# Delta heads: ten products ahead of the first head, queries' bank emptied in hop 3, gate product and second half of the system matrix later

## What is computed

```python
def gated_deltanet(h, w_in, conv_w, a_log, dt_bias, o_norm_g, w_out):
    proj = h @ w_in                                  # queries, keys, values, gate per head
    qkv = silu(causal_dwconv(qkv, conv_w))           # four taps
    q = l2norm(q) * (GDN_DK ** -0.5);  k = l2norm(k)
    kk = einsum('bhcid,bhcjd->bhcij', kc, kc)
    tri = where(strict, b * kk * decay, 0) + eye     # the system matrix
    sol = triangular_solve(tri, rhs)                 # the kernel inverts tri
    def step(S, inp):                                # over the chunks, in order
        v_new = u_c - w_c @ S
        o = qd_c @ S + qk_c @ v_new
        S = cd_c * S + kd_c.T @ v_new
    o = rmsnorm(o, o_norm_g) * silu(gate)            # the gate product
    return o @ w_out
```

## Time and profile before

| what | value |
|---|---|
| median of three runs | 2954.01 us (2953.73 to 2957.56) |
| profiled execution, time | 2953.93 us |
| profiled execution, span | 2952.2 us |
| granted TensorE clock, mean | 0.996 |
| busy: PE, DVE, ACT, POOL | 98%, 72%, 43%, 24% |
| delta heads in the span | from 1660.84 us (first P4) on; 454.56 us from the P4 of head 1 to the P4 of head 7 |

### The profile page before, as it was taken

How to read it: one execution, slowest core, us unless ns; L and a number is a source line. 1 busy time by engine, 2 the same in 40 slices (tenths; PEclk the granted TensorE clock), 3 DMA queues, 4 the chain that set the end, 5 groups by cost and what they waited for, 6 DMA issues and landing times.

```text
span 2952.2 us, 41363 instructions
## 1 busy us (share of the span) xinstructions
PE 2902.3 (98%) x14190; PEld 2409.8 (82%) x14190; DVE 2131.2 (72%) x2591; ACT 1257.9 (43%) x1857; POOL 720.9 (24%) x1126
## 2 busy tenths in 40 slices
PE   8999999999999999999899999999999999999998
PEld 7888887878888888887787788888887888878887
DVE  6665669858686868687886666666665667788887
ACT  4121124345454545455445454455453433344444
POOL 1000000014444444445001322222221356630000
PEclk9999999999999999999999999999999999999999
DMA  4213236332111211122532211111112344465542
GB/s 108 93 58 99 85 80 217 117 100 58 46 50 43 64 46 50 44 63 89 200 129 52 90 40 40 39 39 39 39 53 75 117 159 153 151 230 164 157 157 86
DMA packets 346911, 274.34 MB, mean 93 GB/s; under 512 B 82232, under 2 KB 297272, under 8 KB 342976
## 3 DMA queue, kind: packets, MB, share of 16 engines
q1 hardware_dynamic: 345664, 273.05, 30.1%
q10 hardware_dynamic: 1152, 0.07, 0.0%
HBM read 197.80 MB, written 75.27 MB: 92 GB/s over the span
## 4 chain that ended last, share of the span: by engine, by line
PE 89%; DVE 5%; issue 2%; DMA 1%; POOL 1%; ACT 1%; SPq 0%; DVEq 0%; POOLq 0%; ACTq 0%
PE banks L1105 9%; PE banks L1107 9%; PE banks L1106 9%; PE banks L1003 5%; PE banks L1005 5%; PE banks L1004 5%; PE banks L1087 3%; PE banks L1088 3%; PE banks L1089 3%; PE banks L1499 3%; PE banks L1500 3%; PE banks L1498 3%; PE banks L1590 3%; PE banks L1592 3%; PE banks L1591 3%; PE banks L1132 2%
## 5 line engine op out<-in xcount | busy, mean ns | idle before, releaser
L1105 PE MATMUL banks<-state_a_hi,weights_hi 128*128 128x512 f32 x1280 | 539.7, 422 | 0.9 <-DVE weights_lo L2221 0.8
L1107 PE MATMUL banks<-state_a_hi,weights_lo 128*128 128x512 f32 x1280 | 504.0, 394 | 0.0
L1106 PE MATMUL banks<-state_a_lo,weights_hi 128*128 128x512 f32 x1280 | 501.0, 391 | 0.0
L1107 PEld LDWEIGHTS banks<-state_a_hi,weights_lo 128*128 128x128 f32 x1280 | 240.3, 188 | 54.4
L1105 PEld LDWEIGHTS banks<-state_a_hi,weights_hi 128*128 128x128 f32 x1280 | 241.6, 189 | 39.5 <-issue 2.0
L1106 PEld LDWEIGHTS banks<-state_a_lo,weights_hi 128*128 128x128 f32 x1280 | 242.3, 189 | 34.0 <-issue 0.5
L831 POOL TENSOR_TENSOR beta<-beta,stick_left 128x128 f32<-128x128 f32 (+1 forms) x192 | 169.5, 883 | 393.0 <-DVE stick_left L2458 391.0
L2458 DVE TENSOR_TENSOR_SCAN stick_left<-stick_left,eps_column 128x128 f32<-128x128 f32 (+1 forms) x192 | 237.1, 1235 | 29.5 <-POOL beta L826 23.1
L2221 DVE TENSOR_TENSOR weights_lo<-weights_raw,weights_hi 128x1024 fp32r<-128x1024 f32 x133 | 180.6, 1358 | 80.6 <-ACT weights_hi L1618 68.2
L1618 ACT ACTIVATE weights_hi<-weights_raw 128x1024 fp32r<-128x1024 f32 x133 | 140.1, 1053 | 194.2 <-PE banks L1005 155.7
L1003 PE MATMUL banks<-state_a_hi,weights_hi 128*128 128x512 f32 x536 | 208.8, 389 | 1.5 <-DVE stream_again L2756 1.5
(11 more groups left out here) (532 smaller groups left out, 7327.8 us busy)
## 6 DMA issues: line engine op xcount, KB each, us to landing
weights_raw<-in_mlp_w_dram SPq DMA_DIRECT2D x34, 512.0 KB, 5.6
weights_raw<-in_gdn_w_in_dram SPq DMA_DIRECT2D x33, 512.0 KB, 4.1
weights_raw<-in_pool_w_in_dram SPq DMA_DIRECT2D x32, 512.0 KB, 4.1
state_a_lo<-relu_blocks_dram SPq DMA_DIRECT2D x16, 1024.0 KB, 7.1
weights_raw<-in_sb_w_in_dram SPq DMA_DIRECT2D x32, 512.0 KB, 4.1
relu_blocks_dram<-relu_sums SPq DMA_DIRECT2D x16, 1024.0 KB, 4.3
state_b_lo<-relu_blocks_dram SPq DMA_DIRECT2D x16, 1024.0 KB, 8.8
down_weights_raw<-in_mlp_w_dram SPq DMA_DIRECT2D x30, 512.0 KB, 5.3
```

Of the source, the lines that this page charges most:

```text
L1105: pe.matmul(psum[:, bank, :], whi, hi, start=(k == 0), stop=False)
L1106: pe.matmul(psum[:, bank, :], whi, lo, start=False, stop=False)
L1107: last = pe.matmul(psum[:, bank, :], wlo, hi, start=False, stop=(k == end - 1))
```

## The change

1. PE, way in: the last two products of T2 come after the keys' sums of squares; T3's products around `scores_k` are cut 4 and 4 (6 and 2 before); T4's first four products come ahead of the queries' sums of squares, its other twelve behind; the transposed keys and the scores come after all of T4. `AHEAD` is 10: eight products of T5's first half and two of its second before P4. `IN_INVERSE` stays, so T6 (the gate) begins in hop 4 and hops 7 and 8 hold no product.
2. DVE and ACT, way in: order of evacuations, taps and rescalings changed to fit; ACT makes three small exponentials after the keys' norm instead of before.
3. DVE, every head: queries' first bank is emptied at n = 3 (5 before), with the wait for the keys' taps; the keys' second bank before the wait for the root of the output (n = 0 of the next head before).
4. DVE, every head: P1_4 of the next head stands between y1 and y2, and y2 has a semaphore of its own.
5. DVE, every head: NT1 is at n = 17 (15 before), behind St3.

```diff
-        AHEAD, IN_INVERSE = KC - 2, (2, 1, 2, 1, 2, 1, 1)
+        AHEAD, IN_INVERSE = KC + 2, (2, 1, 2, 1, 2, 1, 1)
...
-            return [(x // KC, x % KC) for x in range(2 * KC, 8 * KC)
+            return [(x // KC, x % KC) for x in range(AHEAD + sum(IN_INVERSE), 8 * KC)
...
-            gemm_part(base[0], 1, 0, KC, A)
+            gemm_part(base[0], 1, 0, 6, A)
...
-                    for k in range(AHEAD):
-                        gemm_part(tile_at[0], 0, k, k + 1, A)
+                    for x in range(AHEAD):
+                        gemm_part(tile_at[0], x // KC, x % KC, x % KC + 1, A)
...
             for h in range(2):
                 norm_sum("k", h, 7 - h)
+            gemm_part(base[0], 1, 6, KC, A)
             base[0] = tile.fixed
-            gemm_part(base[0], 0, 0, 6, A)
+            gemm_part(base[0], 0, 0, 4, A)
             for h in range(2):
                 scores_k(h, 7 - h)
-            gemm_part(base[0], 0, 6, KC, A)
+            gemm_part(base[0], 0, 4, KC, A)
             gemm_part(base[0], 1, 0, KC, A)
+            base[0] = tile.fixed
+            gemm_part(base[0], 0, 0, 4, A)
             for h in range(2):
                 norm_sum("q", h, 7 - h)
-            base[0] = tile.fixed
-            gemm_part(base[0], 0, 0, KC, A)
+            gemm_part(base[0], 0, 4, KC, A)
+            gemm_part(base[0], 1, 0, KC, A)
             turn_k()
             scores()
-            gemm_part(base[0], 1, 0, KC, A)
             head("first")
...
             act.preload_act_table_set(LN_EXP)
+            decays()
+            norm_roots("k", (7, 6))
+            decay_rows()
             act.wait_ge(pre_dve, PRE["dl"])
...
-            decays()
-            norm_roots("k", (7, 6))
-            decay_rows()
             split_weights(halves.value())
...
             square_rest("k")
-            dve.wait_ge(pre_act, PRA["eg"])
-            did("neg", dve.tensor_scalar(eg_s[:, :, :], eg_s[:, :, :], -1.0, None, ALU.mult))
-            after("neg")
-            evac(1)
-            tap(qT, 0, slice(0, 1))
+            rescale(2, 3)
...
+            def level_step(l):
+                ev.wait("pe", f"P{l}")
+                ev.did(f"P1_{l}", dve.tensor_tensor(P1[:, :, :], psum[:, 4, :].rearrange("p (c n) -> p c n", n=64),
+                                                   lmask[:, l - LEVEL0:l - LEVEL0 + 1, :].to_broadcast([P, TT, 64]), ALU.mult))
             def head(kind, e):
-                ev.next[0] = 0
+                ev.next[0] = 1
...
-                    if n == 0:
+                    if n == 9:
                         evac(1)
-                    if n in (5, 9):
-                        evac((n - 5) // 4)
...
-                    if n in (4, 16, 29):
+                    if n == 3:
+                        dve.wait_ge(conv_done, cdn.add())
+                        evac(0)
+                    if n in (16, 29):
                         dve.wait_ge(conv_done, cdn.add())
...
-                    if n in (13, 15):
-                        system((n - 13) // 2)
+                    if n in (13, 17):
+                        system((n - 13) // 4)
...
+                if kind == "full":
+                    evac(1)
...
-                ev.wait("dve", "y1")
+                y1_done = ev.at("dve", "y1")
+                if kind != "last":
+                    ev.head = e + 1
+                    level_step(LEVEL0)
+                dve.wait_ge(*y1_done)
                 dve.wait_ge(stream_saved, 32)
                 yb = y_g[:, one(e), :].rearrange("p a n -> p (a n)")
-                ev.did("y2", dve.scalar_tensor_tensor(out=yb, in0=flat(oT), scalar=o_gain[:, :], in1=(kT if kind == "last" else gT)[:, :], op0=ALU.mult, op1=ALU.mult))
-                ev.wait("dve", "y2")
+                dve.scalar_tensor_tensor(out=yb, in0=flat(oT), scalar=o_gain[:, :], in1=(kT if kind == "last" else gT)[:, :],
+                                         op0=ALU.mult, op1=ALU.mult).then_inc(head_mixed, 1)
+                dve.wait_ge(head_mixed, e + 1)
+            evac(1)
             normed_k()
-            tap(qT, 1, slice(0, 1))
+            tap(qT, 0, slice(0, 1))
             for h in range(2):
                 system(h, 7 - h)
-            for i in range(2, TAPS):
+            for i in range(1, TAPS):
                 tap(qT, i, slice(0, 1))
+            dve.wait_ge(pre_act, PRA["eg"])
+            did("neg", dve.tensor_scalar(eg_s[:, :, :], eg_s[:, :, :], -1.0, None, ALU.mult))
+            after("neg")
             split_weights()
             dve.wait_ge(conv_done, 2)
             evac(0)
+            rescale(3, 4)
             square_rest("q")
...
             dve.wait_ge(conv_done, 3)
+            evac(0)
             split_weights()
+            evac(1)
             k_to_end(0)
             scores_decayed()
             q_decayed()
-            evac(0)
             ev.wait("pool", "xb")
-            rescale(2, KC)
+            rescale(4, KC)
+            level_step(LEVEL0)
```

More of the change, by code:

```diff
@@ L251, in build @@
         yg_hi, yg_lo = sem("delta_y_hi"), sem("delta_y_lo")
+        head_mixed = sem("delta_head_mixed")
         block_hi, block_lo = sem("relu_sums_hi_done"), sem("relu_sums_lo_done")
@@ L263, in build @@
         DVE_MAIN = ([f"{x}{l}" for l in range(LEVEL0, LEVELS) for x in ("P1_", "X_")]
-                    + [f"{x}{c}" for c in range(TT) for x in ("R", "vw", "St") if (c or x != "R") and (c < TT - 1 or x != "St")] + ["oT", "olo", "y1", "y2"])
+                    + [f"{x}{c}" for c in range(TT) for x in ("R", "vw", "St") if (c or x != "R") and (c < TT - 1 or x != "St")] + ["oT", "olo", "y1"])
         ACT_MAIN = ["XT3", "vn", "XT4", "XT5", "osq", "ohi", "oln", "ors"]
@@ L1945, in fill @@
                         if n == OUT_K - 1:
-                            act.wait_ge(*y2_of_head_6)
+                            act.wait_ge(head_mixed, HEADS - 1)
                         if n < OUT_K:
@@ L2034, in _ @@
                 head("full")
-            ev.head = HEADS - 2
-            y2_of_head_6 = ev.at("dve", "y2")
             ev.head = HEADS - 1
             head("last")
-            ev.wait("dve", "y2")
+            act.wait_ge(head_mixed, HEADS)
             round_mixed(HEADS - 1)
@@ L2809, in head @@
                     w = 1 << l
-                    ev.wait("pe", f"P{l}")
-                    ev.did(f"P1_{l}", dve.tensor_tensor(P1[:, :, :], psum[:, 4, :].rearrange("p (c n) -> p c n", n=64),
-                                                       lmask[:, l - LEVEL0:l - LEVEL0 + 1, :].to_broadcast([P, TT, 64]), ALU.mult))
+                    if l > LEVEL0:
+                        level_step(l)
                     fill(n); n += 1
```

## The result

The kernel after takes 2965.12 us (median; 2962.68 to 2967.76), the kernel before, on the same chip, 2954.96 us. The ratio is 1.0034, with a 95% interval of 1.0023 to 1.0044: slower by 10 us, in the upper half of the range given. The profiled executions have spans of 2964.2 and 2952.2 us, 12.0 us apart. Lines of the kernel after are numbered one higher than before around P4 (L1379) and S (L1413), NT is L2735.

What follows compares the result with a forecast made beforehand. PE, busy 98%, was taken as the bound, with the inverted blocks' chain nearly as late: 2953.9 + 7.0 us (0.3 to head 1's P4, 6.7 in heads 1 to 6) + 1.4 for half clock = 2962.3 us; range 2950 to 2970.

Steps and rivals of the forecast that it cites:

- the likeliest case: Whole kernel: the forecast itself, 2962.3 us, by itself spanning 2957 to 2967 us, chance 0.60; slower had chance 0.67.
- The slack and NT1's delay: Heads: blocks stored 1.53 us later, only slack of 0.12 to 0.57 us per head free (2.23 us over six), rest idle PE.
- Part 3: DVE, heads 2 to 5: P1_4 ahead of y2 removes 0.3 us of Q4's wait per head, 1.2 us in all.
- The rival with more slack: Heads: slack larger than read, so the blocks cost PE nothing and 6.5 us is gained, 2947.5 us; chance 0.12.
- POOL's +0.16 per head: POOL's inversion: steps laid out anew against DVE's taps end 1.69 us later for a 1.53 us delay, 0.16 us more.
- The same term in head 0: Head 0's inversion for head 1's P4: 0.1 us on top of NT1's 1.53 us delay, P4 0.3 us later in all.
- The half clock in head 1: After head 1's P4: 2.8 us of idle time may bring half clock, 0 to 2.83 us; 1.4 us taken.
- vw's wait: S3 in heads 0 to 6: wait for vw gone, 0.47 us each, 3.3 us in all, hidden by NT1's delay.
- The way in: Before head 0: NT1 some 1.0 us earlier, inversion's end and head 0's P4 0.96 us earlier, bounds 0.6 to 1.2.
- The wait for T6's weights in hop 4: Head 0: PE waits for DVE's rest of T6's weights in hop 4, priced at 1.4 us, about 1.1 us expected in the trace.
- four products ahead: Head 0: four products (2.7 us) pay for the hop 4 wait and the bare chain, leaving 0.3 us, bounds -1 to +1.5.
- The rival of the clock at each head's border: Before P4 of heads 2 to 7: idle times of 1.6 to 2.1 us lower the clock, about 2969 us; chance 0.15.

Runs made afterwards that it cites:

- Experiment 1: Kernel after with only NT1 moved back to n = 15, the rest of the change kept: 2954.29 us, ratio 0.9996 to the kernel before.
- experiment 2: Kernel before with NT1 moved to n = 17 and nothing else changed: 2967.95 us, ratio 1.0040.
- experiment 4: Kernel after, NT1 still late, with the last four of the 28 steps in POOL's inversion loop left out: 2952.61 us, ratio 0.9987.
- experiment 9: Kernel after with fourteen matmuls nobody reads at the end of head 0, filling PE's idle time before head 1's P4: 2964.96 us, ratio 1.0034.
- experiment 3: Kernel after with NT1 at n = 14, one turn earlier than in the kernel before: 2953.71 us, ratio 0.9994.
- experiment 5: Kernel after with NT1 back at n = 15 and eight products ahead instead of ten: 2953.70 us, ratio 0.9999.
- experiment 6: Kernel after with NT1 back at n = 15 and six products ahead instead of ten: 2953.72 us, ratio 1.0001.
- experiment 7: Kernel after with DVE's rest of the weights two turns later, n = 20 instead of 18: 2994.6 us, ratio 1.0134.
- experiment 10: Kernel after with NT1 at n = 14, eight products ahead and DVE's rest of the weights at n = 20: 2948.13 us, ratio 0.9976.

## Why the prediction was right, and where its terms were off

Forecast 2962.3 us, measured 2965.1, inside the range; slower, as the likeliest case had it. Against the span the forecast had 8.4 us more and the trace shows 12.0 (10.2 in the medians). By stretches, counted from the matmul that sums the decays in the way in (1615.48 before, 1615.95 after): head 0's P4 0.44 us earlier (forecast 0.96), head 0 longer by 3.42 us (forecast 1.3), heads 1 to 6 longer by 7.96 us (forecast 6.7 and 1.4 for the clock), the rest 1.1 us outside the heads. Four of these were forecast too low (0.5 us in the way in, 2.2 in head 0, 1.7 for the clock, 1.1 outside) and one too high (1.9 in heads 1 to 6). That the sum came within 3 us of the median is in part luck: the cause and the sign were right, the sizes partly cancel.

**The slack and NT1's delay: right.** From P4 to the store it is 47.85 us in head 1, half clock included, and in heads 2 to 5 44.72 for 43.47: 1.25 us later, which is the forecast 1.53 less the 0.3 of Part 3. In head 6, which has nothing of Part 3, it is 44.62 for 43.03, 1.59 later. (From S3 to St3 I took 0.75 us where the earlier trace rows give 0.84 and the kernel after 0.83; that is within the bounds.) Experiments 1 and 2 show that this is the loss, and experiment 4 that it acts through POOL's chain. The rival with more slack is refuted: P4 of all of heads 2 to 7 waits for the DMA.

**POOL's +0.16 per head: wrong.** From the store to the load it is 26.76 to 26.78 us in heads 1 to 5, where before it was 26.65 and 27.07 in turn. Over heads 1 to 6 this took 0.55 us less, where I had 0.96 more. The slack was also larger than the 2.23 us: P4 of heads 2 to 7 starts 5.12 us behind the load in the mean, not 5.22, and 2.8 us were used up. So without the clock these heads lost 4.8 us, not 6.7.

**The same term in head 0** was wrong the other way: there POOL took 19.48 us for 17.53, and its 1.95 us are the largest part of why head 1's P4 came 3.45 us later and not 0.3. I had priced the lock from one step and carried it to all heads alike, while the trace has the chain in head 0 at another place against DVE's operations.

**Part 3: right.** From P4 to Q4 it is 4.1 us in heads 2 to 5, where it was 4.4, and 4.1 or less in heads 1, 6 and 7 already before: four heads and 1.1 us for the forecast 1.2. Experiment 1 takes 452.75 us for heads 1 to 6 where the kernel before takes 454.56; where the other 0.7 us come from, no run shows.

**The half clock in head 1: right in kind, taken at half.** I gave 1.4 us out of 0 to 2.83. With 3.96 us of idle time instead of the forecast 2.8 it came in full: 3.1 us by experiment 9's stretch, and 3.1 us again from P4 to the store (47.85 for 44.73).

**vw's wait: wrong, without a price here.** I had it gone at S3. It is gone there, and stands at S4, seven times 0.5 us, since vw4 is queued behind a wait for ACT. I named what stood ahead of vw3 and did not read on to vw4. It cost nothing while the chain set P4, but it is what kept experiment 3 from its forecast.

**The way in: half right.** NT1 ended 1.0 us earlier, as worked out. From the first store to the load back it then took 4.90 us for 4.43, and that took half of it; 0.44 of 0.96 arrived, below the bound of 0.6. POOL's part, from which I had taken the lower bound, is as long as before (19.93 and 19.89 us). The wait for T6's weights in hop 4 is there, 1.04 us for 1.1 to 1.4:

```profile
1680.88 1.22 DVE L2222 TENSOR_TENSOR weights_lo<-weights_raw,weights_hi 128x1024 fp32r<-128x1024 f32 x1
...
1682.15 0.50 PE L1106 MATMUL banks<-state_a_hi,weights_hi 128*128 128x512 f32 x1 [1.04 <-DVE weights_lo L2222]
```

That four products ahead are worth almost nothing is confirmed by experiments 5 and 6: ten instead of six give -0.8 us (a loss) from P4 to P4 where I had +0.3, inside the bounds of -1 to +1.5.

**The rival of the clock at each head's border** did not happen here, where the idle times of heads 2 to 7 are 0.46 to 0.78 us, and did in experiment 7. The forecast itself had put them at 1.6 to 2.1. It had the inverse 0.3 us later in each head than it came, and it took vw's wait, 0.47 us a head, out of PE's work, where it stayed.

## What to carry to other kernels

Before an operation on a second engine is moved by one turn, follow the chain that it starts to the next place where the first engine needs it, and take the slack from the time between the last transfer's issue and the use: here 5.22 us of need against 5.3 to 5.8 us of room, while the waits showed nothing. Where such a chain is the bound, taking small waits away elsewhere brings nothing and can cost, and the same edits pay once the chain has slack. Where an idle stretch ahead of a long run of matmuls can't be avoided, matmuls without a use, as many as end before the awaited operand comes, keep the clock up.

## What the runs showed of the hardware that was not expected

A chain of small POOL steps changes its length by its place alone: 17.5, 18.8 and 19.5 us for the same 28 steps in heads of one size (kernel after, experiments 10 and 7). The Trainium skill, "SBUF — State Buffer", section "Terms", says of the port pair shared by VectorE and GpSimd that the loser of the lock blocks for the whole of the other's instruction. The rows of experiment 7 agree, with 1.26 us for a step of 0.28 that ended just behind VectorE's operation.

In head 0 a store or a load of the blocks lands later than in head 1: from the first store to POOL's start it is 8.2 to 8.4 us for 7.0 to 7.1, in the four kernels named below. Before the change it is the load back to SBUF that is late (3.4 us to landing for 2.1), after it one of the stores (2.9 for 1.5). In each of the four (before, after, and experiments 1 and 6) a packet of instructions lies in that microsecond on a DMA queue of its own, as in the microsecond from 1708 us of the kernel after (packets, MB, share):

```profile
q8 instruction: 1, 0.02, 7.6%
```

In head 1 of the kernel after there is none, and the landings are 1.5 and 2.1 us. That this packet delays the transfer is only argued; no run moved it. It hits both kernels and is no part of the difference.
